# Finishing attention heads 0 to 3 inside the last units, starting the output projections on half of the heads, and starting the value projection from the first tile

## The chip, the core and the metric

The kernel runs on one core of a Trainium2 chip. The core has a matrix engine (PE, TensorE), three engines for vectors and scalars (DVE, ACT, POOL) and a queue engine (SP) that issues most transfers. Each engine works through its own list of instructions in order; semaphores tie the lists together. Times are device microseconds of one execution; lower is better.

## What is computed

The reference is a decoder of two layers over 512 tokens of width 1024. Layer 0 is a convolution module, layer 1 an attention that mixes three dilated windows; each is followed by a mixture of experts (64 experts, 8 for each token). Cut to what the change touches:

```python
def conv_module(x, w_in, b_in, w_dw, b_dw, ln_g, ln_b, w_out, b_out):
    ...
    h = jax.nn.silu(layernorm(h, ln_g, ln_b))
    return h @ w_out + b_out

def dilated_mixture_attention(x, positions, w_q, w_o, k, v):
    q = rotary((x @ w_q).reshape(B, S, N_GROUPS, HEADS_PER_GROUP, HEAD_DIM), positions)
    for g, (win, dil) in enumerate(WINDOW_DILATIONS):   # (128, 1), (512, 4), (2048, 16)
        o, lse = dilated_window_attention(q[:, :, g], k[:, :, g], v[:, :, g], dil, steps)
        ...
    wts = jax.nn.softmax(jnp.stack(lses, axis=2), axis=2)
    o = jnp.einsum("bsgh,bsghd->bshd", wts, jnp.stack(outs, axis=2))
    return o.astype(x.dtype).reshape(B, S, ATTN_OUT_WIDTH) @ w_o
```

Keys and values come from `x @ w_kv`. The result of each module is added to alpha times x and normalised (`layernorm`), then the experts run and a second norm follows.

## The kernel before

The 512 tokens are 4 tiles of 128 (`NT`), n = 0 to 3; the width is 8 pieces of 128 (`KT`). All engines run the same sequence of stages: the convolution, its output projection and norm round 0, the experts of layer 0 (a loop over blocks of 128 rows), norm round 1, the value projection, 16 attention units, the mixing of the heads, the attention's output projection and norm round 2, the experts of layer 1, norm round 3. PSUM has 8 banks (`PS[:, 0]` to `PS[:, 7]`).

**Norm rounds.** `norm_round(r)` on DVE normalises one tile after another (L876 residual, only in rounds 0 and 2; L884 statistics, L889 and L890 scale and shift, about 5 us in all). `x_T` on PE (L1233) transposes the tile; ACT and DVE copy it out. In round 1 ACT writes the rounded part `XTH` and DVE the remainder `XTL` (L861); DVE does this for tile n behind the norm of tile n+1.

**Value projection** (L1448 on PE). 24 pieces of weights, 3 buffers (`PIECES`). SP loads a piece into `RAW`, ACT rounds it into `PH` (L778), DVE takes the remainder `PL` (L1118). A product is three matmuls, so that float32 keeps its precision. PE takes piece by piece, in each all 4 tiles; it begins when all 4 tiles are transposed. Query and key pieces (48 more) follow on the same three buffers.

**Attention units.** Units 0 to 7 are the heads of the near window (one projection pair each), units 8 to 15 the heads of both dilated windows together (two pairs, `items(u)`). PE's list for unit u: `project(u+1)` (L1464), `probs_T(u-1)` (L1489, transposes of the probabilities), `scores(u)` (L1477), `pv(u-1)` (L1502). DVE rotates queries and keys, then masks the scores and takes the row maximum (L1165 to L1167), and copies the result of `pv` out (L1173). ACT copies the projections out (L799), computes the exponentials (L809) and copies the transposed probabilities (L814, L815).

**Mixing.** Near heads have tokens as rows in their order, dilated ("far") heads in another. So the row maxima and sums are exchanged through a small array in memory, `stat_ex`: SP issues two stores, waits, and issues two loads (L451 to L455), behind the last softmax. Then DVE and ACT work out the weights for all 8 heads (L1190 to L1200, L835), DVE scales the near and the far results (L1204), PE transposes them (L1530), ACT copies the near ones into `OT` (L840), DVE adds the far ones (L1213).

**Output projections.** `out_proj(l, ...)` runs after all of this for layer 1, and for layer 0 after all 8 pieces of the activated convolution (`s_z`, ACT L767). Each of the 64 float32 products (L1246; the trace shows two matmul records for one) reads its weights' chunk from `W`. Tile n uses banks 2(n % 2) and the next, so tile 2 waits for norm 0.

## Time and profile before

| | us |
| --- | --- |
| median of 3 runs | 2486.32 |
| lowest and highest | 2479.92, 2489.36 |
| the profiled execution's own time | 2482.47 |
| its span, first to last instruction | 2480.7 |
| PE busy | 2296.2 (93% of the span) |
| DVE busy | 1606.8 (65%) |
| ACT busy | 1076.4 (43%) |
| POOL busy | 684.8 (28%) |

The profile cuts the span into 40 slices. PE shows 9 tenths or more in nearly all of them; the lower ones lie at the start, at about slice 17 (around 1060 us), at slice 25 (around 1560 us) and after the second output projection. The stages that the change touches lie at 190 to 255 us, 1050 to 1219 us and 1540 to 1645 us.

### The profile page before, as it was taken

Reading aid. Unit: us, or ns where it says so; the run is one execution under the profiler, and the core shown is the slowest. Engines: PE = TensorE matmul, PEld = TensorE weight load, DVE = VectorE, ACT = ScalarE, POOL = GpSimd, SP = SyncE. Lnnn points to the kernel's source line nnn. Section 1 sums busy time; section 2 is a strip of 40 time slices with the busy share of each in tenths; the row PEclk is TensorE's granted clock in tenths of the full one; section 3 lists DMA queues with packets and bytes.
Section 4 is the critical chain, followed back from the end, with each engine's and each line's share of the span. In section 5 each row is a group of like instructions: output and inputs, shape, how many; then the busy total and the mean of one; then the engine's idle time right before and its main releaser. Section 6 shows DMA issues by size and latency. Waiting matters only on the chain.

```text
span 2480.7 us, 32934 instructions
## 1 busy us (share of the span) xinstructions
PE 2296.2 (93%) x9437; PEld 1633.7 (66%) x9437; DVE 1606.8 (65%) x1737; ACT 1076.4 (43%) x1215; POOL 684.8 (28%) x698
## 2 busy tenths in 40 slices
PE   7948889999999999869999999798999999999994
PEld 4413557767666667559988888554667777676673
DVE  4874557777767667552377787436677777776675
ACT  3651135555555555422243333112555555555552
POOL 3970213443434333200000000002233433334331
PEclk9969889999999999979999999889999999999997
DMA  6210359999999999633322222132999999999994
GB/s 216 68 34 0 127 202 346 371 366 375 360 350 362 365 345 372 209 134 93 94 77 69 79 83 83 56 119 70 339 366 367 368 364 363 367 372 355 360 364 142
DMA packets 197117, 592.57 MB, mean 239 GB/s; under 512 B 26605, under 2 KB 96277, under 8 KB 161732
## 3 DMA queue, kind: packets, MB, share of 16 engines
q1 hardware_dynamic: 165140, 517.92, 56.0%
q0 software_dynamic: 31920, 73.91, 12.2%
q8 instruction: 33, 0.54, 0.1%
q14 instruction: 24, 0.20, 0.0%
HBM read 579.16 MB, written 51.38 MB: 254 GB/s over the span
## 4 chain that ended last, share of the span: by engine, by line
PE 81%; DVE 6%; DMA 4%; ACT 1%; issue 1%; POOLq 0%; SPq 0%; DVEq 0%; ACTq 0%
PE PS L1355 29%; PE PS L1376 18%; PE PS L1464 11%; PE PS L1448 5%; PE PS L1246 5%; PE PS L1342 5%; DMA W<-in_exp_w_down 4%; PE PS L1280 2%; PE PS L1477 1%; PE PS L1364 1%; PE PS L1502 1%; PE PS L1326 1%; DMA acc<-BIG,IDXS 1%; PE PS L1299 1%; PE PS L1489 1%
## 5 line engine op out<-in xcount | busy, mean ns | idle before, releaser
L998 DVE TENSOR_TENSOR WL<-W,WH 128x2048 fp32r<-128x2048 f32 x276 | 621.3, 2293 | 197.3 <-ACT WH L679 185.9
L679 ACT ACTIVATE WH<-W 128x2048 fp32r<-128x2048 f32 x276 | 512.4, 1907 | 43.1 <-DVE IDX L976 42.4
L1376 PE MATMUL PS<-W,BIG 128*128 128x512 f32 x1104 | 498.6, 594 | 11.1 <-issue 5.0
L1355 PE MATMUL PS<-WH,XH 128*128 128x512 f32 x1104 | 446.6, 405 | 8.8 <-DVE XL L991 8.8
L1355 PE MATMUL PS<-WH,XL 128*128 128x512 f32 x1104 | 435.2, 394 | 0.0
L1355 PE MATMUL PS<-WL,XH 128*128 128x512 f32 x1104 | 432.6, 392 | 0.0
L589 POOL DMA_INDIRECT acc<-BIG,IDXS x138 | 259.1, 1878 | 471.3 <-issue 371.3
L1376 PEld LDWEIGHTS PS<-W,BIG 128*128 128x128 f32 x1104 | 199.2, 190 | 212.8 <-issue 205.1
L1355 PEld LDWEIGHTS PS<-WH,XH 128*128 128x128 f32 x1104 | 209.7, 190 | 48.2 <-DVE XL L991 9.6
L689 ACT ACTIVATE BIG<-PS 128x512 f32<-128x512 f32 x138 | 82.5, 598 | 362.5 <-PE PS L1376 362.5
L1355 PEld LDWEIGHTS PS<-WH,XL 128*128 128x128 f32 x1104 | 209.2, 189 | 46.0
L1355 PEld LDWEIGHTS PS<-WL,XH 128*128 128x128 f32 x1104 | 209.9, 190 | 39.7
L1016 DVE COPY BIG<-PS 128x512 f32<-128x512 f32 x138 | 95.4, 692 | 193.1 <-PE PS L1376 193.1
L528 POOL MEMSET BIG<- 128x2048 f32 x2 | 3.6, 1804 | 693.2 <-DVE X L890 601.4
L991 DVE TENSOR_TENSOR XL<-PS,XH 128x1024 fp32r<-128x1024 f32 x138 | 169.0, 1225 | 38.7 <-ACT XH L673 38.1
L574 POOL DMA_INDIRECT BIG<-xrows,IDXG x138 | 150.6, 1091 | 124.5 <-POOL IDXG L571 115.5
L673 ACT ACTIVATE XH<-PS 128x1024 fp32r<-128x1024 f32 x138 | 141.3, 1024 | 71.4 <-PE PS L1342 68.4
L1118 DVE TENSOR_TENSOR PL<-RAW,PH 128x1024 fp32r<-128x1024 f32 x72 | 87.5, 1217 | 114.7 <-ACT PH L778 114.7
L580 POOL COPY IDXS<-IDX 128x1 uint32 (+1 forms) x138 | 84.1, 609 | 250.9 <-issue 250.8
L1342 PEld LDWEIGHTS PS<-ident,BIG 128*128 128x128 f32 x1104 | 142.9, 188 | 15.8 <-issue 4.7
L1464 PE MATMUL PS<-XTH,PH 128*128 128x512 f32 x384 | 150.7, 393 | 0.0
L1464 PE MATMUL PS<-XTH,PL 128*128 128x512 f32 x384 | 149.6, 390 | 0.0
(233 smaller groups left out, 3110.2 us busy)
## 6 DMA issues: line engine op xcount, KB each, us to landing
W<-in_exp_w_gate SPq DMA_DIRECT2D x138, 1024.0 KB
W<-in_exp_w_up SPq DMA_DIRECT2D x138, 1024.0 KB
W<-in_exp_w_down SPq DMA_DIRECT2D x138, 1024.0 KB
RAW<-in_w_kv SPq DMA_DIRECT2D x48, 512.0 KB, 3.8
RAW<-in_attn_w_q SPq DMA_DIRECT2D x24, 512.0 KB, 3.7
W<-in_conv_w_in SPq DMA_DIRECT2D x8, 1024.0 KB, 11.4
acc<-BIG SPq DMA_DIRECT2D x9, 512.0 KB, 3.7
W<-in_conv_w_out SPq DMA_DIRECT2D x4, 1024.0 KB, 6.5
```

The source lines that it names most:

```text
L574: pool.indirect_dma_start(XG[:, s, :], None, xrows, bass.IndirectOffsetOnAxis(IDXG[:, s:s + 1], axis=0), bounds_check=T - 1, oob_is_err=Fa ...
L589: pool.indirect_dma_start(acc, bass.IndirectOffsetOnAxis(IDXS[0:r, s:s + 1], axis=0), YB[0:r, s, :], None, compute_op=ALU.add).then_inc(s_ ...
L673: A(XH[:, s, :], PS[:, 0:2, :].rearrange("p a t -> p (a t)"), ACT.Copy).then_inc(s_xh[l], 1)
L679: A(WH[:, s, c, :], W[:, 3 - 3 * s + c, :], ACT.Copy).then_inc(s_wh[l], 1)
L991: v.tensor_tensor(XL[:, s, :], PS[:, 0:2, :].rearrange("p a t -> p (a t)"), XH[:, s, :].bitcast(F32), ALU.subtract).then_inc(s_xl[l], 1)
L998: v.tensor_tensor(WL[s][:, c, :], W[:, 3 - 3 * s + c, :], WH[:, s, c, :].bitcast(F32), ALU.subtract).then_inc(s_wl[l], 1)
L1246: last = mm(PS[:, 2 * (n % 2) + h, :].rearrange("p (a b) -> p a b", a=2), lhs[:, k, n * P:(n + 1) * P], pair((key, 2 * h), k), start=(k == ...
L1342: last = nc.tensor.transpose(PS[:, k // 4, (k % 4) * P:(k % 4 + 1) * P], XG[:, s, :].rearrange("p (c k) -> p k c", k=KT)[:, k, :], ident[: ...
L1355: last = mm(PS[:, 3 + s, :].rearrange("p (a b) -> p a b", a=2), a, w, start=(k == 0 and i == 0), stop=(k == KT - 1 and i == 2))
L1376: last = mm(PS[:, 5 + h, :], HTm[:, s, k * P:(k + 1) * P], wd[:, k, h * 512:(h + 1) * 512], start=(k == 0), stop=(k == 1))
L1448: last = mm(PS[:, 4 * (c % 2) + n, :], a, w, start=(k == 0 and i == 0), stop=(k == KT - 1 and i == 2))
L1464: last = mm(PS[:, w, :], a, b[:, k, :], start=(k == 0 and t == 0), stop=(k == KT - 1 and t == 2))
```

## The change

1. **Layer 0 output projection.** Tiles 0 and 1 are worked on together, one piece k of the activations at a time, each as soon as that piece is ready. Tiles use four bank pairs (2n), so that no tile waits for a norm.
2. **Value projection.** The first three pieces are made (`PH`, `PL`) ahead of norm round 1 and are used tile by tile, as soon as that tile is transposed. The norm vectors' load (`ln_vectors(2)`) moves from piece 3 to piece 9 in SP's list.
3. **Heads 0 to 3 ("half 0").** Their weights, scaling and transposes are placed inside units 13 to 15. The statistics go out and come back in three exchanges, issued by POOL, the last with heads 4 to 7 alone. The near heads are scaled on ACT, the far ones on DVE.
4. **End of the units.** `scores(15)` uses banks 0 and 1 and stands ahead of `probs_T(14)`.
5. **Layer 1 output projection.** The products of tiles 0, 1 and 2 with heads 0 to 3 (24 of 64) stand between the transposes of heads 4 to 7; the other 40 follow.

The diff, cut to its core:

```diff
+        def xt_bank(q):
+
+            r, n = q // NT, q % NT
+            return 2 * n if r % 2 else 4 + 2 * (n % 2)
+
+        OT4 = BIG[:, 4096:8192].rearrange("p (m f t) -> p f m t", m=4, f=2)
+
+        MIX = 2 * 2 + 2 + NT
...
-                if j == PIECES:
+                if j == 3 * PIECES:
...
+            pool.wait_ge(s_p, 4 * 12)
+            pool.wait_ge(s_m, 12)
+            pool.dma_start(stat_ex[1].rearrange("(i j) c -> i j c", j=NT)[:, :, 0:8], statP[:, 1, :, 0:8]).then_inc(s_so, 16)
+            pool.wait_ge(s_so, 32)
+            pool.dma_start(statN[:, 1, :, 0:8], stat_ex[1].rearrange("(n p) c -> p n c", p=P)[:, :, 0:8]).then_inc(s_si, 16)
+            pool.wait_ge(s_p, 4 * 16)
+            pool.wait_ge(s_m, 16)
+            pool.dma_start(stat_ex[1].rearrange("(i j) c -> i j c", j=NT)[:, :, 8:16], statP[:, 1, :, 8:16]).then_inc(s_so, 16)
+            pool.wait_ge(s_so, 48)
+            pool.dma_start(statN[:, 1, :, 8:16], stat_ex[1].rearrange("(n p) c -> p n c", p=P)[:, :, 8:16]).then_inc(s_si, 16)
...
-            for j in range(PIECES - 1):
+            for j in range(PIECES):
                 piece_high(j)
+            norm_round(1)
             for j in range(n_v):
-                piece_high(j + PIECES - 1)
+                if j >= 1:
+                    piece_high(j + PIECES - 1)
...
+            def near_weigh(hf, n):
+                act.wait_ge(s_dve_w, MIX * hf + 5)
+                for h in range(4 * hf, 4 * hf + 4):
+                    o = O0[:, n, h * P:(h + 1) * P]
+                    last = A(o, o, ACT.Copy, scale=wt[:, 0, 3, n, h:h + 1])
+                last.then_inc(s_wn, 1)
+
+            def near_T(hf, n):
+                act.wait_ge(s_ot, 8 * hf + n + 1)
+                bank = 7 if hf == 0 else 6 + n % 2
+                A(OT4[:, hf, :, n * P:(n + 1) * P], PS[:, bank, :].rearrange("p (h t) -> p h t", h=4),
+                  ACT.Copy).then_inc(s_otn, 1)
...
+            def beside(u):
+
+                if u == 14:
+                    return lambda i: near_weigh(0, i - 1) if i else None
+                if u == 15:
+                    return lambda i: near_T(0, i)
+                return lambda i: None
...
+            def far_weigh(hf, n):
+                dve.wait_ge(s_dve_w, MIX * hf + 6)
+                o = O12[:, n, 512 * hf:512 * hf + 512].rearrange("p (h c) -> p h c", h=4)
+                v.tensor_tensor(o, o, wt[:, 1, 3, n, 4 * hf:4 * hf + 4].unsqueeze(2).broadcast_to([P, 4, P]),
+                                ALU.mult).then_inc(s_dve_w, 1)
+
+            def far_T(hf, n):
+                dve.wait_ge(s_otn, 4 * hf + 4)
+                dve.wait_ge(s_ot, 8 * hf + NT + n + 1)
+                bank = 7 if hf == 0 else 6 + n % 2
+                src = PS[:, bank, :].rearrange("p (h t) -> p h t", h=4)
+                dst = OT4[:, hf, :, :].rearrange("p h (i j) -> p h j i", j=NT)[:, :, n, :]
+                v.tensor_tensor(dst, dst, src, ALU.add).then_inc(s_ote, 1)
...
+            for u in range(16):
+                for k, (i, g) in enumerate(items(u)):
+                    rotate(i, g, u % 2, k, beside(u))
+                if u == 13:
+                    mix_least(0)
+            row_max(15)
+            far_T(0, 0)
+            far_T(0, 1)
+            pv_copy(14)
+            far_T(0, 2)
+            far_T(0, 3)
+            mix_least(1)
+            mix_weights(1, 0)
+            mix_weights(1, 1)
...
-            def out_proj(l, lhs, key):
-
-                for c in range(4):
-                    landed(pe, (key, c))
-                for n in range(NT):
-                    if n >= 2:
-                        pe.wait_ge(s_norm, 2 * NT * l + n - 1)
-                    for h in range(2):
-                        for k in range(KT):
-                            last = mm(PS[:, 2 * (n % 2) + h, :].rearrange("p (a b) -> p a b", a=2),
-                                      lhs[:, k, n * P:(n + 1) * P], pair((key, 2 * h), k), start=(k == 0), stop=(k == KT - 1))
-                    last.then_inc(s_mix[l], 1)
-                    if n >= 2:
-                        x_T(NT * (2 * l + 1) + n - 2)
+            def out_part(l, n, ks, hs=(0, 1)):
+
+                key = ("co", "ao")[l]
+                for h in hs:
+                    for k in ks:
+                        lhs = Y[:, k, :] if l == 0 else OT4[:, k // 4, k % 4, :]
+                        last = mm(PS[:, 2 * n + h, :].rearrange("p (a b) -> p a b", a=2),
+                                  lhs[:, n * P:(n + 1) * P], pair((key, 2 * h), k), start=(k == 0), stop=(k == KT - 1))
+                return last
+
+            def out_rest(l):
+
+                out_part(l, 2, range(4 if l else 0, KT)).then_inc(s_mix[l], 1)
+                x_T(NT * (2 * l + 1))
+                out_part(l, 3, range(KT)).then_inc(s_mix[l], 1)
+                x_T(NT * (2 * l + 1) + 1)
...
-            pe.wait_ge(s_z, KT)
-            out_proj(0, Y, "co")
+            for c in range(4):
+                landed(pe, ("co", c))
+            for k in range(KT):
+                pe.wait_ge(s_z, k + 1)
+                for n in range(2):
+                    last = out_part(0, n, (k,))
+                    if k == KT - 1:
+                        last.then_inc(s_mix[0], 1)
+            out_rest(0)
...
+            x_T(2 * NT)
+            x_T(2 * NT + 1)
             for n in range(NT):
+                pe.wait_ge(s_xta, 2 * NT + n + 1)
+                pe.wait_ge(s_xtv, 2 * NT + n + 1)
+                for j in range(PIECES):
+                    if n == 0:
+                        pe.wait_ge(s_pl, j + 1)
+                    last = v_part(j, n)
+                    if n == NT - 1:
+                        last.then_inc(s_v, 1)
+                if n + 2 < NT:
+                    x_T(2 * NT + n + 2)
...
+            def heads_T(hf, far, n):
+
+                f = NT * far + n
+                if far:
+                    pe.wait_ge(s_dve_w, MIX * hf + 6 + n + 1)
+                else:
+                    pe.wait_ge(s_wn, 4 * hf + n + 1)
+                if hf == 0:
+                    if f > NT:
+                        pe.wait_ge(s_ote, f - NT)
+                    elif f >= 1:
+                        pe.wait_ge(s_otn, f)
+                    bank = 7
+                else:
+                    if f < 2:
+                        pe.wait_ge(s_oe, 16)
+                        pe.wait_ge(s_ote, NT)
+                    elif f < 2 + NT:
+                        pe.wait_ge(s_otn, NT + f - 1)
+                    else:
+                        pe.wait_ge(s_ote, f - 1)
+                    bank = 6 + n % 2
+                o = (O0, O12)[far]
+                for h in range(4):
+                    last = nc.tensor.transpose(PS[:, bank, h * P:(h + 1) * P],
+                                               o[:, n, (4 * hf + h) * P:(4 * hf + h + 1) * P], ident[:, :])
+                last.then_inc(s_ot, 1)
...
+                        if u == 15:
+                            heads_T(0, 0, 2 * m + w)
...
+            for u in range(15):
+                project(u + 1)
                 if u >= 1:
                     probs_T(u - 1)
                 scores(u)
                 if u >= 1:
                     pv(u - 1)
+            scores(15)
+            heads_T(0, 1, 0)
+            probs_T(14)
+            heads_T(0, 1, 1)
+            pv(14)
+            heads_T(0, 1, 2)
             probs_T(15)
+            heads_T(0, 1, 3)
             pv(15)
-            for c in range(2 * NT):
-                o, n = (O0, O12)[c // NT], c % NT
-                pe.wait_ge(s_wts, c + 1)
-                if 2 <= c < NT + 2:
-                    pe.wait_ge(s_otn, 2 * (c - 1))
-                elif c >= 2:
-                    pe.wait_ge(s_ote, 2 * (c - 1 - NT))
-                for hf in range(2):
-                    for h in range(4):
-                        last = nc.tensor.transpose(PS[:, 4 + 2 * (c % 2) + hf, h * P:(h + 1) * P],
-                                                   o[:, n, (4 * hf + h) * P:(4 * hf + h + 1) * P], ident[:, :])
-                    last.then_inc(s_ot, 1)
+            pe.wait_ge(s_ote, NT)
+            for c in range(4):
+                landed(pe, ("ao", c))
+            out_part(1, 0, range(4))
+            heads_T(1, 0, 0)
+            heads_T(1, 0, 1)
+            out_part(1, 1, range(4), (0,))
+            heads_T(1, 0, 2)
+            heads_T(1, 0, 3)
+            out_part(1, 1, range(4), (1,))
+            heads_T(1, 1, 0)
+            heads_T(1, 1, 1)
+            out_part(1, 2, range(4), (0,))
+            heads_T(1, 1, 2)
+            heads_T(1, 1, 3)
+            out_part(1, 2, range(4), (1,))
             pe.wait_ge(s_ote, 2 * NT)
-            out_proj(1, OT, "ao")
+            for n in range(2):
+                out_part(1, n, range(4, KT)).then_inc(s_mix[1], 1)
+            out_rest(1)```

Three places show how the lists change. The names are those of buffers: `X` the tiles, `PL<-RAW,PH` the remainder of a weight piece, `XTL` the remainder of the transposed tile. First DVE before, at the end of norm round 1: the norm of the fourth tile, then the pieces.

```order
L884 BN_STATS bns<-X 128x6 x2
L886 BN_AGGR mv<-bns 128x2
L888 RECIPROCAL rstd<-std 128x1
L889 SCALAR_TENSOR_TENSOR X<-X,mv,LNG 128x1024
L890 SCALAR_TENSOR_TENSOR X<-X,rstd,LNB 128x1024
L861 TENSOR_TENSOR XTL<-PS,XTH 128x8x128 x2
L1112 TENSOR_SCALAR sinT<-sinT,sgn 32x512
L1118 TENSOR_TENSOR PL<-RAW,PH 128x1024 x6
```

DVE in the changed kernel, at the start of norm round 1, directly behind the last copy of the experts (L1066):

```order
L1066 COPY BIG<-PS 128x512
L1161 TENSOR_SCALAR sinT<-sinT,sgn 32x512
L1167 TENSOR_TENSOR PL<-RAW,PH 128x1024 x3
L934 BN_STATS bns<-X 128x6 x2
L936 BN_AGGR mv<-bns 128x2
L938 RECIPROCAL rstd<-std 128x1
L939 SCALAR_TENSOR_TENSOR X<-X,mv,LNG 128x1024
L940 SCALAR_TENSOR_TENSOR X<-X,rstd,LNB 128x1024
```

The first three pieces moved ahead of the first tile's norm. Next PE before, from `probs_T(14)` to `pv(15)`: transposes of probabilities (`PS<-ident,BIG`), scores and the product with the values (both `PS<-BIG`).

```order
L1489 MATMUL PS<-ident,BIG 128x128 x8
L1477 MATMUL PS<-BIG 128x128 x8
L1502 MATMUL PS<-BIG 128x128 x8
L1489 MATMUL PS<-ident,BIG 128x128 x8
L1502 MATMUL PS<-BIG 128x128 x8
```

PE in the changed kernel at the same place (L1617 is `scores(15)`, L1629 `probs_T`, L1642 `pv`, L1587 a `heads_T` of four far heads):

```order
L1617 MATMUL PS<-BIG 128x128 x8
L1587 MATMUL PS<-ident,BIG 128x128 x4
L1629 MATMUL PS<-ident,BIG 128x128 x8
L1587 MATMUL PS<-ident,BIG 128x128 x4
L1642 MATMUL PS<-BIG 128x128 x8
L1587 MATMUL PS<-ident,BIG 128x128 x4
L1629 MATMUL PS<-ident,BIG 128x128 x8
L1587 MATMUL PS<-ident,BIG 128x128 x4
L1642 MATMUL PS<-BIG 128x128 x8
```

The scores of unit 15 moved ahead of `probs_T(14)`, and four transposes of finished heads came in. Last PE before, from the heads' transposes to the end of the output projection (`PS<-W,BIG`):

```order
L1530 MATMUL PS<-ident,BIG 128x128 x64
L1246 MATMUL PS<-W,BIG 128x512 x48
L1233 MATMUL PS<-ident,X 128x128 x8
L1246 MATMUL PS<-W,BIG 128x512 x16
L1233 MATMUL PS<-ident,X 128x128 x16
```

PE in the changed kernel at the same place:

```order
L1329 MATMUL PS<-W,BIG 128x512 x8
L1587 MATMUL PS<-ident,BIG 128x128 x8
L1329 MATMUL PS<-W,BIG 128x512 x4
L1587 MATMUL PS<-ident,BIG 128x128 x8
L1329 MATMUL PS<-W,BIG 128x512 x4
L1587 MATMUL PS<-ident,BIG 128x128 x8
L1329 MATMUL PS<-W,BIG 128x512 x4
L1587 MATMUL PS<-ident,BIG 128x128 x8
L1329 MATMUL PS<-W,BIG 128x512 x28
L1319 MATMUL PS<-ident,X 128x128 x8
L1329 MATMUL PS<-W,BIG 128x512 x16
L1319 MATMUL PS<-ident,X 128x128 x16
```

Half of the 64 transposes left this place (they stand in units 15 and behind), and 20 of the 64 products stand ahead of the last of the others.

## Rows read from the trace of the kernel before

**Rows 1.** Stretches of the span: length, busy time (count) of each engine, granted clock, DMA share, GB/s.

```profile
1083.00:1219.00 136.00, 135.86 (x576) 127.84 (x577) 36.90 (x35) 29.25 (x33) 0.00 (x0) 0.98 0.33 101
1540.00:1586.00 46.00, 28.14 (x171) 26.07 (x169) 30.11 (x46) 14.26 (x36) 0.00 (x0) 0.78 0.45 140
```

**Rows 2.** Timeline (start, length, engine, line, [idle before]), end of the convolution.

```profile
190.85 5.75 ACT L767 ACTIVATE BIG<-BIG,vecT 128x512 f32<-128x512 f32 x8 [2.85 <-DVE BIG L1107]
196.65 43.24 PE L1246 MATMUL PS<-W,BIG 128*128 128x512 f32 x96 [10.77 <-ACT BIG L767]
```

**Rows 3.** Timeline, norm round 1 and the start of the value projection.

```profile
1054.65 1.53 SPq L445 DMA_DIRECT2D RAW<-in_w_kv  x3
1056.24 1.29 DVE L884 BATCH_NORM_STATS2 bns<-X 128x6 f32<-128x512 f32 x2 [9.48 <-DMA X<-acc]
...
1060.99 1.97 PE L1233 MATMUL PS<-ident,X 128*128 128x128 f32 x8 [15.05 <-DVE X L890]
...
1065.46 1.22 DVE L861 TENSOR_TENSOR XTL<-PS,XTH 128x1024 fp32r<-128x1024 f32 x1
...
1079.99 2.94 ACT L778 ACTIVATE PH<-RAW 128x1024 fp32r<-128x1024 f32 x3
...
1081.77 3.50 DVE L1118 TENSOR_TENSOR PL<-RAW,PH 128x1024 fp32r<-128x1024 f32 x3
...
1083.14 0.77 PE L1448 MATMUL PS<-PH,XTH 128*128 128x512 f32 x1 [4.11 <-DVE PL L1118]
```

**Rows 4.** DMA issues from 1055.5 to 1056.3: size, median us to landing.

```profile
RAW<-in_w_kv SPq DMA_DIRECT2D x2, 512.0 KB, 9.3
```

**Rows 5.** First projection of queries and keys: duration ns, first and last start.

```profile
L1464 PE MATMUL PS<-XTH,PH x384: 389/389/476, 1219.2 to 1539.7; 128*128 128x512 f32 x192
```

**Rows 6.** Timeline, units 14 and 15 and the exchange.

```profile
1540.41 1.03 PE L1489 MATMUL PS<-ident,BIG 128*128 128x128 f32 x8
1541.28 1.95 PE L1477 MATMUL PS<-BIG 128*128 128x128 f32 x16
...
1544.70 1.21 DVE L1165 TENSOR_TENSOR PS<-PS,mask_far 128x1024 f32<-128x1024 f32 x1
...
1547.41 0.47 ACT L809 ACTIVATE BIG<-PS,statP 128x256 f32<-128x256 f32 x1 [4.85 <-DVE statP L1167]
...
1549.39 1.97 PE L1489 MATMUL PS<-ident,BIG 128*128 128x128 f32 x8 [4.38 <-ACT BIG L809]
...
1551.16 3.62 PE L1477 MATMUL PS<-BIG 128*128 128x128 f32 x16
...
1559.50 0.37 SPq L451 DMA_DIRECT2D stat_ex<-statN  x1
...
1561.80 3.47 PE L1502 MATMUL PS<-BIG 128*128 128x128 f32 x16 [1.17 <-ACT BIG L815]
...
1565.30 0.69 DVE L1173 COPY BIG<-PS 128x512 f32<-128x512 f32 x1 [7.21 <-PE PS L1502]
1565.91 0.18 DVE L1190 TENSOR_TENSOR wt<-statN 128x32 f32<-128x32 f32 x1
```

**Rows 7.** Timeline, mixing, all 8 heads.

```profile
1569.23 6.90 DVE L1204 TENSOR_TENSOR BIG<-BIG,wt 128x1024 f32<-128x1024 f32 x6
...
1578.32 7.92 DVE L1213 TENSOR_TENSOR BIG<-BIG,PS 128x512 f32<-128x512 f32 x8
```

**Rows 8.** Timeline of PE, output projection of layer 1.

```profile
1586.30 43.03 PE L1246 MATMUL PS<-W,BIG 128*128 128x512 f32 x96 [2.02 <-DVE BIG L1213]
...
1630.04 13.90 PE L1246 MATMUL PS<-W,BIG 128*128 128x512 f32 x32
1643.78 1.91 PE L1233 MATMUL PS<-ident,X 128*128 128x128 f32 x16
```

**Rows 9.** Timeline: last indirect transfer of POOL, and SP's loads that wait for it.

```profile
1048.71 1.38 POOL L589 DMA_INDIRECT acc<-BIG,IDXS  x1 [2.50 <-issue]
1052.84 1.76 SPq L412 DMA_DIRECT2D X<-acc  x4
```

More of the change, by code:

```diff
@@ L769, in _ @@
             moe(0)
-            norm_round(1)
             def piece_high(j):
@@ L1441, in _ @@
                 pe.wait_ge(s_pl, j + 1)
[L1442 to L1448 removed]
+                for n in range(NT):
+                    last = v_part(j, n)
                 last.then_inc(s_v, 1)
@@ L1510, in _ @@
             pe.wait_ge(s_veh, 12)
-            for u in range(16):
-                if u < 15:
-                    project(u + 1)
+            for u in range(15):
+                project(u + 1)
                 if u >= 1:
```

171 lines of the change are left out of this document (91 added, 80 removed).

## The prediction

> **What bounds the kernel now.** I read the page first: PE is busy for 93% of the span, so a change pays only where PE waits or where its list gets shorter. Then I cut the span into stretches. In the value projection PE has 135.86 us of work in 136; between the last projection and the output projection it has 28.14 in 46, at a granted clock of 0.78 [rows 1]. The timelines of the three touched places then show what ends each wait. The convolution's output projection starts at 196.65, when the last of 8 activations ends [rows 2]. The value projection starts at 1083.14, behind four norms and the first pieces; its first tile was normed by 1060.99 [rows 3]. The output projection of layer 1 starts at 1586.30, 45.9 us after PE ended its last projection at 1540.41 [rows 6, 8]. The experts' loops, most of the span, are not touched; what the three places save should reach the end one for one, because every later stage hangs on PE's or the norm's end.
>
> **Part 1, layer 0 output projection: 5 us.** Eight activations take 5.75 us [rows 2], 0.72 from start to start, so the first is ready 7 x 0.72 = 5.0 us ahead of the last. A piece k gives PE four products. 32 records took 13.90 us [rows 8], so a product (two records) takes 0.87 and four 3.5, five times as long as one activation: once PE has begun it is never starved. The number of products is the same. Norm 0 now comes after tile 1 instead of tile 0, but two norms of about 7 us lie under the 14 us of tile 2 and more under tile 3; the end, tile 3's norm, moves with tile 3. Gain 5.0; bounds 3.5 (a slow start of the clock lasting longer because the work ahead is further away) and 5.0.
>
> **Part 2, value projection: 2 us.** Norm round 1 now stands behind three pieces on DVE. SP issues them right behind X, from 1054.65 to 1056.18 [rows 3], and the later two take 9.3 us to land in the median [rows 4], so the third is there at about 1065.4. ACT's rounding takes 1.0 and DVE's remainder 1.2 more [rows 3], with hand-overs 1067.8. Norm 0, which began at 1056.24, is 11.6 us later. From its start the first transposed tile took 4.8 (1060.99), and its remainder begins 9.2 and ends 10.4 after the start (1066.68) [rows 3]: now 1078.3. PE has tile 1's transposes to finish first, until 1079.1. There the projection starts, 4.0 us earlier than 1083.14. But two transposed tiles (8 transposes each, 1.03 as in [rows 6]) now lie inside it: 2.1 us. A tile's share of three pieces is 18 matmuls, at 135.86 / 576 = 0.236 [rows 1] 4.2 us, and with its transposes 5.3, while DVE brings a tile every 5.7 us (a norm 4.5, a remainder 1.2) and has a lead of one tile. Piece 4 is needed 4.2 us after tile 3's share begins; its buffers come free after the first third (1.4), and rounding and remainder take 2.2: just in time. The queries' projection, now at 1219.2 [rows 5], comes at about 1217.2. Gain 2; bounds -2 (pieces land 2 us later, or the last tiles wait for DVE) and +5 (pieces 3 us earlier). This is the part where the change works against itself: it frees PE of the wait for four norms and puts the norms behind a load.
>
> **Part 3, end of the units and layer 1 output projection: 19 us.** E is the end of PE's last projection, 1540.4. Four groups of four transposes (half of 1.03 each) are inserted in `project(15)`, three ahead of E: E moves to 1542.0 [rows 6]. The work on heads 0 to 3 on DVE (six steps, about 6 us) lies in unit 14, where DVE has some 4.5 of 26 us free; it comes late by about 1.5 us, and PE wants its pieces two steps (11 us) later, so I price it at nothing; without that cover it would cost those 1.5.
>
> From E: the rotation ends and the row maximum starts at +4.3 as before (1544.70) [rows 6]. `scores(15)` no longer waits for unit 14's softmax, +5.2 to +7.1; row maximum of 14, a copy, row maximum of 15 (2.6 each) end at +10.2. Softmax 14 is over at +8.9, `probs_T(14)` at +10, its copies at +11.3, softmax 15 at +13.2, i.e. 1555.2; before 1559.50, where the exchange begins [rows 6]. Then transposes of probabilities, copies, `heads_T(0,1,3)` and `pv(15)`: PE is free at +18.6, and I add 1.5 because `pv(15)` took 3.47 instead of 1.95 at the lower clock [rows 6]: B = 1562.1.
>
> Behind B PE has 64 products, 56.6 us (1586.30 to 1643.78 less one transposed tile of 0.9) [rows 8], eight groups of transposes 4.1 and one tile 0.9: 61.6. If it never waits, tile 3 ends at 1623.7, against 1643.78: 20.1 less.
>
> Does it wait? The exchange of heads 4 to 7 starts at 1555.2 on POOL. SP's took 1559.50 to 1565.9 at most (DVE went on at 1565.91, maybe behind its copy) [rows 6], so 6.4 or less for two transfers. POOL's last indirect transfer took 4.1 from its start to the release of SP (1048.71 to 1052.84) [rows 9], so twice 8.2. It holds 512 short lines and now meets the six 1 MB weight loads in flight. Lower bound 5, upper 20; I take 10, near the indirect row. DVE starts mixing at 1565.3; half the weights take as long as all (3.3 us, 1565.91 to 1569.23, since they are small steps) [rows 6, 7], the near ones 2.2. ACT scales 4 x 128 columns for a tile; its 256-column step takes 0.47 [rows 6], so a step costs 0.25 to 0.47, a tile 1.0 to 1.9. The first near tile is ready at 1568.7, and PE asks for it after 8 products, 1562.1 + 7 + 0.7 = 1569.8. The transposed near heads are copied only when all four tiles are scaled, at 1571.5 to 1575.1 plus 0.6; PE asks for the first at 1569.8 + 1.0 + 3.5 = 1574.3. So there is no wait at ACT's low price and 1.4 us at its high one; I take 1. The far side (DVE scaling 4 x 0.6, adding 4 x 0.99 [rows 7]) has 4 us of room. Gain 20.1 - 1 = 19; bounds 10 (exchange 20 us: 9 us more wait) and 23 (no loss of clock, exchange hidden). Behind the exchange on DVE stands only the mixing, on POOL nothing until the experts, and SP loses four transfers.
>
> A rule speaks against this part. Before, no transfer of POOL's queue ran beside DVE's work on the mix, and no row shows what one does there. The Trainium skill (SBUF — State Buffer, "Who interferes with whom") says that POOL cannot write the descriptors of its transfers while DVE runs in a two-port mode, as a float32 copy within SBUF does, and that such a transfer goes from some 0.6 to 3.1 us. The DVE steps in this stretch read PSUM, so I expect it not to bite; by its figure the exchange would take 5 us more (an estimate from that page), and the part would gain about 14.
>
> **Sum.** 5 + 2 + 19 = 26. Against the profiled execution's own 2482.47 (1.8 beyond its span) that is 2456.5; against the median of the runs, 3.9 higher, 2460.3. I forecast 2458, between the two. Within 0.5% (12.4 us) a measurement of this kernel can hardly tell a difference from none.
>
> **Rivals.**
> 1. *The forecast: all three parts, 20 to 32 us less.* Chance 0.72: 2450 to 2466.
> 2. *The exchange becomes PE's wait.* DVE waits for POOL's transfers, PE for DVE and ACT. It bites from about 10 us; at 20 it costs 9: total gain 16 to 20, time 2466 to 2472. For: no row shows such a transfer, and the weight loads are in flight. Against: the indirect one took 4.1. Chance 0.12.
> 3. *The early start of the values costs instead of paying, and unit 14 overloads DVE.* Pieces land at 1068, tile 1's norm comes late, PE waits 4 us in the values and some 5 in `project(15)`: gain 12 to 16, time 2468 to 2474. For: DVE's margin in unit 14 is negative by itself. Chance 0.08.
> 4. *No change that can be measured.* The parts gain 5 and 2, and the third only what the earlier softmax gives (4), because PE stays cold or waits between all the small groups: 11 us less, 2475. Against: 24 products of 0.87 are real work taken into the wait, and nothing in the rows starves them all. Chance 0.05.
> 5. *Slower.* POOL's exchange alone: the part's gain is gone at 10 + 19 = 29 us, and all of it at 36; from about 48 us the kernel is slower by 0.5%. At 50 us it would take 2500. Chance 0.01. Another 0.02 for a gain over 32 (colder clock before than I count, 2445).
>
> **Numbers.** The range reaches from 2448 to 2470: it holds the forecast, half of rival 2 and part of 3. Faster by over 0.5%: 0.92; within: 0.06; slower: 0.02.
>
> **What the profile of the changed kernel would show.** Part 1 is right if the first product of layer 0 starts 5 us ahead of the last activation's end, with no gaps. Part 2: the norm's first statistics at about +11.6 and the first value product at 4 us earlier relative to the end of the experts; wrong if norm 0 starts later or PE has gaps between the tiles' shares. Part 3: PE's stretch from the last projection to the end of tile 3's products 81 to 84 us instead of 103.4; softmax 15 some 13 us after the last projection; POOL's two transfers in 10 us. The prediction fails if the products on heads 0 to 3 have gaps among them, if `project(15)` waits for `PL`, or if the transposes between them run at half clock throughout.

## The result, and the profile after

The changed kernel takes 2452.8 us (median of 4 runs, 2450.3 to 2456.2) against 2485.0 for the kernel before (4 runs, 2479.9 to 2489.4): a ratio of 0.987, 95% interval 0.986 to 0.989. The time is in the range (2448 to 2470), 5 us under the forecast of 2458. The profiled execution has a span of 2451.5 us against 2480.7, 29.3 us less.

I cut both traces at the same points of the program. Starts and ends are read from PE's rows, lengths are differences of them (us):

| stretch | before | after | difference |
|---|---|---|---|
| start of the span to the first product, layer 0 output projection | 196.65 | 191.80 | -4.9 |
| from there to the last tile of that projection | 57.69 | 58.93 | +1.2 |
| routing of layer 0 | 94.23 | 95.03 | +0.8 |
| experts' loop of layer 0 | 704.27 | 705.43 | +1.2 |
| SP's load of `X` to the first value product | 30.30 | 25.62 | -4.7 |
| value projection | 136.03 | 136.82 | +0.8 |
| projections of queries and keys with the units among them | 321.40 | 323.26 | +1.9 |
| last of those to the last tile of layer 1's output projection | 103.21 | 77.91 | -25.3 |
| routing, experts' loop and end of layer 1 | 836.96 | 836.67 | -0.3 |

Windows of the changed kernel's trace first (length, then busy time and count of PE, PEld, DVE, ACT, POOL, then granted clock, DMA share, GB/s). The first row begins with the layer 0 output projection, the second with the value projection; the others answer to [rows 1], and the last is the router's stretch.

```profile
191.80:201.80 10.00, 10.00 (x17) 4.23 (x18) 3.22 (x6) 6.07 (x8) 0.00 (x0) 0.69 0.01 2
...
1076.81:1086.81 10.00, 10.00 (x46) 8.26 (x45) 9.07 (x14) 2.42 (x4) 0.00 (x0) 0.91 0.00 1
...
1077.00:1213.00 136.00, 135.98 (x591) 127.82 (x591) 45.66 (x47) 32.71 (x38) 0.00 (x0) 0.99 0.31 95
...
1536.70:1554.80 18.10, 14.60 (x125) 13.70 (x124) 14.04 (x17) 8.10 (x24) 0.72 (x1) 1.00 1.00 317
1554.80:1614.80 60.00, 59.54 (x170) 28.38 (x169) 26.69 (x47) 10.24 (x29) 0.77 (x1) 1.00 0.04 11
1614.80:1640.00 25.20, 22.95 (x107) 17.79 (x106) 11.28 (x29) 4.93 (x7) 1.80 (x1) 0.73 0.82 292
```

The 46 us with 28 us of PE work in them have become 18 with 14.6, at full clock, and the output projection behind them has no hole but one of 0.46 us. In the trace before, the same ten microseconds had a clock of 0.82 and 19 records at the start of the output projection, and 0.77 and 35 records at the start of the value projection.

The timeline of the changed kernel (start, length, engine, operation, idle before), at the three places, answers to [rows 2], [rows 3, 9] and [rows 6, 8]:

```profile
190.84 5.75 ACT L788 ACTIVATE BIG<-BIG,vecT 128x512 f32<-128x512 f32 x8 [2.85 <-DVE BIG L1157]
191.80 44.48 PE L1329 MATMUL PS<-W,BIG 128*128 128x512 f32 x96 [5.93 <-ACT BIG L788]
...
1063.61 1.06 ACT L798 ACTIVATE PH<-RAW 128x1024 fp32r<-128x1024 f32 x1 [0.22 <-DMA RAW<-in_w_kv]
...
1065.84 1.28 DVE L934 BATCH_NORM_STATS2 bns<-X 128x6 f32<-128x512 f32 x2
...
1076.81 0.78 PE L1534 MATMUL PS<-PH,XTH 128*128 128x512 f32 x1
...
1536.50 0.39 PE L1601 MATMUL PS<-XTH,PL 128*128 128x512 f32 x1
...
1545.74 1.09 PE L1629 MATMUL PS<-ident,BIG 128*128 128x128 f32 x8 [1.74 <-ACT BIG L833]
...
1550.07 0.72 POOL L639 DMA_DIRECT2D stat_ex<-statP  x1 [81.54 <-ACT BIG L833]
...
1552.92 2.05 PE L1642 MATMUL PS<-BIG 128*128 128x128 f32 x16
1554.81 7.03 PE L1329 MATMUL PS<-W,BIG 128*128 128x512 f32 x16
...
1555.97 0.77 POOL L641 DMA_DIRECT2D statN<-stat_ex  x1 [5.18 <-DMA stat_ex<-statP]
1558.38 0.18 DVE L1236 TENSOR_TENSOR wt<-statN 128x16 f32<-128x16 f32 x1 [2.68 <-DMA statN<-stat_ex]
...
1560.24 2.45 ACT L852 ACTIVATE BIG<-BIG,wt 128x128 f32<-128x128 f32 x8 [0.65 <-DVE wt L1250]
...
1562.74 0.66 PE L1587 MATMUL PS<-ident,BIG 128*128 128x128 f32 x4 [0.46 <-ACT BIG L852]
1563.23 3.60 PE L1329 MATMUL PS<-W,BIG 128*128 128x512 f32 x8
...
1614.80 1.91 PE L1319 MATMUL PS<-ident,X 128*128 128x128 f32 x16
```

The first product of layer 0 starts 1.0 us after the first activation. The norm's first statistics stand 14.7 us behind SP's load of `X` (1051.18), against 3.4 before [rows 3, 9]. PE goes from the last projection (it ends at 1536.89) to the first attention product in 17.9 us, and the exchange takes 8.3 us from POOL's start to DVE's first mixing step. PE's last steps of the units and its products on heads 0 to 3, started at 1554.81, cover the exchange and the scaling behind it but for 0.46 us.

### The profile page after: what moved, and what is told of

Same layout as the page of the kernel before. It is cut to its first block, busy times and chain, and to the rows that moved or that the text cites. A ratio compares the mean times of both kernels' runs of the same rounds, so it can differ in the third digit from the quotient of the medians.

```text
span 2451.5 us, 32999 instructions
## 1 busy us (share of the span) xinstructions
PE 2286.8 (93%) x9437; PEld 1623.4 (66%) x9437; DVE 1604.3 (65%) x1753; ACT 1085.8 (44%) x1251; POOL 696.8 (28%) x704
## 4 chain that ended last, share of the span: by engine, by line
PE 79%; DMA 8%; DVE 5%; ACT 1%; issue 1%; SPq 0%; POOLq 0%; POOL 0%; DVEq 0%; ACTq 0%
PE PS L1443 27%; PE PS L1464 18%; PE PS L1601 11%; DMA W<-in_exp_w_down 6%; PE PS L1534 6%; PE PS L1329 4%; PE PS L1430 4%; PE PS L1368 2%; PE PS L1452 1%; PE PS L1642 1%; PE PS L1617 1%; PE PS L1414 1%; DMA acc<-BIG,IDXS 1%; PE PS L1387 1%; PE PS L1348 1%
## 5 line engine op out<-in xcount | busy, mean ns | idle before, releaser
L1464 PE MATMUL PS<-W,BIG 128*128 128x512 f32 x1104 | 499.3, 595 | 10.5 <-issue 4.5
L594 POOL DMA_INDIRECT acc<-BIG,IDXS x138 | 265.8, 1926 | 464.7 <-issue 391.6
L1464 PEld LDWEIGHTS PS<-W,BIG 128*128 128x128 f32 x1104 | 199.2, 190 | 213.4 <-issue 204.8
L1066 DVE COPY BIG<-PS 128x512 f32<-128x512 f32 x138 | 95.4, 692 | 194.6 <-PE PS L1464 193.4
L1167 DVE TENSOR_TENSOR PL<-RAW,PH 128x1024 fp32r<-128x1024 f32 x72 | 87.7, 1218 | 121.7 <-ACT PH L798 121.3
L1601 PE MATMUL PS<-XTH,PH 128*128 128x512 f32 x384 | 151.0, 393 | 0.0
L704 ACT ACTIVATE BIG<-PS 128x256 f32<-128x256 f32 x138 | 53.1, 385 | 219.0 <-PE PS L1443 219.0
L1601 PE MATMUL PS<-XTH,PL 128*128 128x512 f32 x384 | 149.7, 390 | 0.0
## 6 DMA issues: line engine op xcount, KB each, us to landing
RAW<-in_w_kv SPq DMA_DIRECT2D x48, 512.0 KB, 3.8
RAW<-in_attn_w_q SPq DMA_DIRECT2D x24, 512.0 KB, 3.8
acc<-BIG SPq DMA_DIRECT2D x9, 512.0 KB, 3.7
```

Source lines behind the costliest of these rows:

```text
L594: pool.indirect_dma_start(acc, bass.IndirectOffsetOnAxis(IDXS[0:r, s:s + 1], axis=0), YB[0:r, s, :], None, compute_op=ALU.add).then_inc(s_ ...
L1464: last = mm(PS[:, 5 + h, :], HTm[:, s, k * P:(k + 1) * P], wd[:, k, h * 512:(h + 1) * 512], start=(k == 0), stop=(k == 1))
L1601: last = mm(PS[:, w, :], a, b[:, k, :], start=(k == 0 and t == 0), stop=(k == KT - 1 and t == 2))
```

## The experiments

The numbers below are of single profiled runs unless an interval is given; kernels that ran together had a kernel before at 2481 to 2486 us beside them. Since the experts' loops alone vary by some 7 us between runs (last section), a part is judged by the length of its own stretch, and the total is told beside it. A stretch varies as well. The one from PE's last projection to the last tile of layer 1's output projection is unedited in seven runs (the changed kernel, its repetition, parts 1 and 2 taken back, part 3 alone, and two with the pieces behind two norms): 77.9 to 80.1 us, the middle one 78.75. The changed kernel's own profile is the shortest of them, so a difference told against its 77.9 is 0.8 us larger than one against the middle.

**Part 1 taken back.** PE waits for all eight pieces once.

```diff
+            pe.wait_ge(s_z, KT)
             for k in range(KT):
-                pe.wait_ge(s_z, k + 1)
```

> The changed kernel, but the output projection of layer 0 waits for all 8 activations again (bank pairs and order of the products kept). Theory (the early start is what pays in part 1): tile 3's products end at 254.3 instead of 250.7, 3.6 us later, and the time rises by 3.6, to about 2456.8. Rival (the bank pairs, which take away the wait for norm 0, are what pays): no change, 250.7.

2459.6 us. The first product starts at 196.26 and the last tile's transposes at 254.59, against 191.80 and 250.72 in the changed kernel, and an end of 248.2 to 250.3 in the ten other runs that kept part 1. The early start is what pays: 3.9 us against the changed kernel, 4.7 against the middle of the eleven ends with part 1 (249.8). The bank pairs, which this run keeps, pay nothing that shows: it ends at 254.59, the kernel before at 254.34.

**Part 2 taken back.** The norms stand ahead of the pieces on DVE and ACT, PE transposes all four tiles and then projects.

```diff
+            norm_round(1)
             for j in range(PIECES):
                 piece_low(j)
-            norm_round(1)
```

> The changed kernel with part 2 undone: norms first, then the pieces, then the value projection of all tiles. Theory (part 2 by itself is worth the 3.9 us that the two traces show from SP's load of X to the first query projection, 166.4 against 162.5): 166.4 again, time up by 3.9. Rival (it is worth nothing by itself, the 3.9 came from the rest): 162.5 and no change of time.

2456.3 us. From SP's load of `X` to the first projection of queries it takes 166.46 us, as before the change (166.33), against 162.45. That is 4.0 us, twice its term in the sum, of this pair. All the runs say 3.3: the three without part 2 have 165.7 to 166.5 (mean 166.2), the eight that have it as in the changed kernel 161.7 to 163.8 (mean 162.8).

**Part 2 with the pieces behind two norms.** The projection from the first tile on stays, but two norms no longer stand behind the load, on DVE and in the same way on ACT.

```diff
-            for j in range(PIECES):
-                piece_low(j)
             norm_round(1)
...
+                    if r == 1 and n == 1:
+                        for j in range(PIECES):
+                            piece_low(j)
```

> The changed kernel, with the first three pieces taken between the second and the third norm of round 1, on ACT and on DVE. In the changed kernel DVE stands idle for 16.5 us until the first piece is there, while X has landed. Theory (the place of the pieces ahead of all norms gives most of the early start back): the first value product starts 15 us behind SP's load of X instead of 25.6, tile 3's share ends 6 to 7 us earlier, and the time falls by 5 to 7, to about 2447. Rival (PE's list is the bound from the first share on, and its clock falls in the gaps between the shares): under 2 us gained.

2444.1 us. The timeline of this kernel (its line numbers are shifted by one or two):

```profile
1051.31 1.29 DVE L935 BATCH_NORM_STATS2 bns<-X 128x6 f32<-128x512 f32 x2 [8.98 <-DMA X<-acc]
...
1061.67 3.49 DVE L1171 TENSOR_TENSOR PL<-RAW,PH 128x1024 fp32r<-128x1024 f32 x3
...
1063.03 0.77 PE L1536 MATMUL PS<-PH,XTH 128*128 128x512 f32 x1 [0.39 <-DVE PL L1171]
...
1069.82 1.10 PE L1321 MATMUL PS<-ident,X 128*128 128x128 f32 x8 [1.11 <-DVE X L941]
...
1075.56 1.09 PE L1321 MATMUL PS<-ident,X 128*128 128x128 f32 x8 [0.16 <-DVE X L941]
```

The values begin 15.1 us behind the load of `X` and not 25.6; DVE's lead is then too small, so PE waits 1.11 and 0.16 us for tiles 2 and 3, and the projection is 2.7 us longer. What stays is 154.6 us for the stretch, 7.8 under the changed kernel. That is what the order of norms and pieces costs, where the prediction saw the change work against itself.

**Part 3 without the early products.** All the transposed heads first, then every product.

```diff
-            out_part(1, 0, range(4))
-            heads_T(1, 0, 0)
...
+            for far in range(2):
+                for n in range(NT):
+                    heads_T(1, far, n)
             pe.wait_ge(s_ote, 2 * NT)
             for n in range(2):
-                out_part(1, n, range(4, KT)).then_inc(s_mix[1], 1)
+                out_part(1, n, range(KT)).then_inc(s_mix[1], 1)
```

> The changed kernel, but all 64 products of layer 1's output projection stand behind the last transposed heads again; halves, placement of heads 0 to 3 and the order of the units are kept. Theory (the 24 products of 0.86 us lie in a wait for the mixing of heads 4 to 7): PE waits some 16 us between pv(15) and the products, tile 3 ends at 1631 instead of 1614.8, the time rises by 15 to 18. Rival (what pays in part 3 is the work on heads 0 to 3 inside the units, the chain of the second half is short): up by less than 6.

2455.4 us, which is only 2.6 over the changed kernel and misses the total. Its timeline and, in the last row, the window that answers to the last one above:

```profile
1546.55 2.05 PE L1642 MATMUL PS<-BIG 128*128 128x128 f32 x16
1555.30 1.98 PE L1587 MATMUL PS<-ident,BIG 128*128 128x128 f32 x8 [6.71 <-ACT BIG L852]
1559.08 3.81 PE L1587 MATMUL PS<-ident,BIG 128*128 128x128 f32 x16 [1.79 <-ACT BIG L858]
1563.38 2.09 PE L1587 MATMUL PS<-ident,BIG 128*128 128x128 f32 x8 [0.50 <-DVE BIG L1264]
1566.69 43.64 PE L1329 MATMUL PS<-W,BIG 128*128 128x512 f32 x96 [1.22 <-DVE BIG L1264]
...
1624.80:1650.00 25.20, 22.95 (x137) 18.07 (x136) 12.14 (x35) 5.58 (x9) 2.53 (x2) 0.93 0.83 292
```

PE waits 6.71, 1.79, 0.50 and 1.22 us where the changed kernel has products, and runs its transposes at the lower clock (1.98 us for the eight that take 1.04). The stretch from the last projection to the last tile is 94.3 us against 77.9: 16.4 more, as the theory said. The rest of the program happened to be shorter: the routing of layer 1, an unchanged list, took 87.8 us and not 93.1, since the granted clock of its first 25.2 us was 0.93 and not 0.73 (137 records and not 107); the two experts' loops were 7.1 us shorter together. Both runs took their unit steps up to `pv(15)` alike (the slow `pv(14)` told of below is in neither), so the 16 us are a fair difference. That the stage lost them is measured; the total of one run couldn't show it.

**The last exchange on SP's queue**, behind the weight loads that stand there.

```diff
             for i in range(n_first, n_first + SLOTS):
                 load_chunk(i)
+            sp.wait_ge(s_p, 4 * 16)
+            sp.wait_ge(s_m, 16)
+            sp.dma_start(stat_ex[1]..., statP[:, 1, :, 8:16]).then_inc(s_so2, 16)
+            sp.wait_ge(s_so2, 16)
+            sp.dma_start(statN[:, 1, :, 8:16], stat_ex[1]...).then_inc(s_si2, 16)
```

> The changed kernel, with the last exchange of statistics (heads 4 to 7) issued by SP behind its weight loads instead of by POOL. In the changed kernel it takes 8.6 us from the last softmax (1549.77) to the first step of the mixing (1558.38), and PE waits 0.5 us for scaled near heads. Theory (PE is not held up by the exchange, its list is the bound): exchange some 3 us shorter, PE's stretch from its last projection to tile 3's end 77.9 before and 77 to 78 now. Rival (the exchange on POOL is the bound of the second half): 3 us shorter.

2453.3 us. Its timeline:

```profile
1548.09 1.79 SPq L464 DMA_DIRECT2D stat_ex<-statP  x1
...
1556.34 0.37 SPq L466 DMA_DIRECT2D statN<-stat_ex  x1
...
1558.23 0.17 DVE L1241 TENSOR_TENSOR wt<-statN 128x16 f32<-128x16 f32 x1 [4.20 <-DMA statN<-stat_ex]
...
1561.42 0.66 PE L1592 MATMUL PS<-ident,BIG 128*128 128x128 f32 x4 [1.25 <-ACT BIG L854]
```

Expected shorter, it is longer: 10.1 us instead of 8.3, of which the store alone 8.3. PE waits 1.25 and 0.52 us, and its stretch is 79.5 us, forecast 77 to 78. My theory that POOL's path makes the exchange slow fell here.

**The exchange done twice**, on POOL; the mixing waits for the second.

```diff
+            pool.wait_ge(s_si, 48)
+            pool.dma_start(stat_ex[1]..., statP[:, 1, :, 8:16]).then_inc(s_so, 16)
+            pool.wait_ge(s_so, 64)
+            pool.dma_start(statN[:, 1, :, 8:16], stat_ex[1]...).then_inc(s_si, 16)
...
-                dve.wait_ge(s_si, 32 + 16 * hf)
+                dve.wait_ge(s_si, 32 + 32 * hf)
```

> The changed kernel, with the last exchange done a second time by POOL behind the first, with the same data; the mixing waits for the second. It costs 8.3 us more until the mixing starts. Theory (there is next to no room behind the exchange: PE already waits 0.5 us for ACT's scaled near heads): PE's stretch from its last projection to tile 3's end grows from 77.9 to 85.5 to 86.5. Rival (the products between the transposes leave room): under 4 us more.

2451.8 us. The timeline of its POOL, and of PE:

```profile
1542.47 0.72 POOL L639 DMA_DIRECT2D stat_ex<-statP  x1 [81.52 <-ACT BIG L837]
1548.42 0.77 POOL L641 DMA_DIRECT2D statN<-stat_ex  x1 [5.23 <-DMA stat_ex<-statP]
1551.29 0.72 POOL L643 DMA_DIRECT2D stat_ex<-statP  x1 [2.11 <-DMA statN<-stat_ex]
1553.70 0.77 POOL L645 DMA_DIRECT2D statN<-stat_ex  x1 [1.69 <-DMA stat_ex<-statP]
...
1559.13 0.66 PE L1591 MATMUL PS<-ident,BIG 128*128 128x128 f32 x4 [3.33 <-ACT BIG L856]
...
1560.86 5.23 PE L1333 MATMUL PS<-W,BIG 128*128 128x512 f32 x8
```

The first store takes 5.95 us from its start to the next transfer, the identical second one 2.41. So the exchange costs 8.8 us the first time and, with DVE going on at 1555.93, 4.6 the second. PE's stretch grows by 6.9 us to 84.8: its waits are 3.33 and 0.52 instead of 0.46, products that took 3.60 take 5.23 at the lower clock after the wait, and `pv(14)` took 3.06 instead of 1.95. So nearly all added time comes out at PE. How much room there was depends on `pv(14)`: where it took 1.95 us, PE waits already behind an exchange of 8.3; where it was slow, as here, the first product starts 1.5 us later and PE doesn't wait behind the single exchange (so in part 1 taken back and in both runs of the pieces behind two norms). Against those runs (78.75 to 78.9 us) the 5.2 us of longer exchange delay the first transposes by 3.5 and lengthen the stretch by 6.0; 1.6 of that are the eight products of 5.23 us.

**`scores(15)` behind unit 14's transposes again**, as in the kernel before.

```diff
-            scores(15)
             heads_T(0, 1, 0)
             probs_T(14)
+            scores(15)
             heads_T(0, 1, 1)
```

> The changed kernel, with scores(15) behind probs_T(14) again, as in the kernel before. Theory (the softmax of unit 15 and with it both the exchange and pv(15) hang on these scores): softmax 15, the exchange and the first product come 4 us later, PE's stretch from its last projection to tile 3's end grows from 77.9 to about 82. Rival (that order is worth nothing, since DVE's and ACT's steps follow one another anyhow): under 1 us.

2456.9 us. PE in its timeline:

```profile
1541.79 1.70 PE L1629 MATMUL PS<-ident,BIG 128*128 128x128 f32 x8 [3.52 <-ACT BIG L833]
1543.27 3.03 PE L1617 MATMUL PS<-BIG 128*128 128x128 f32 x16
1550.16 1.09 PE L1587 MATMUL PS<-ident,BIG 128*128 128x128 f32 x4 [3.86 <-DVE BIG L1264]
1551.04 3.62 PE L1642 MATMUL PS<-BIG 128*128 128x128 f32 x16
```

The stretch is 86.0 us, 8.1 more (7.3 against the middle of the unedited ones) and not 4: the direction was right, the size about double. PE has two waits of 3.5 and 3.9 us instead of 1.7 and 1.2, and the scores and `pv(14)` behind them take 3.03 and 3.62 instead of 1.95 each. Of the 8.1 us, 4.4 are the longer waits, 2.8 are those two steps at the lower clock, and the rest is spread over small steps.

**The weight loads behind the exchange.** SP issues its first four loads and holds the rest until the exchange is over.

```diff
             for i in range(n_first, n_first + SLOTS):
+                if i == n_first + 4:
+                    sp.wait_ge(s_si, 48)
                 load_chunk(i)
```

> The changed kernel, with SP's loads of the shared experts' gate and up weights (1 MB each) held until the last exchange is over; it is issued by POOL as in the changed kernel. There the first of its two transfers took 5.9 us from issue to landing, and 2.4 when it was repeated later with no load in flight. Theory (the store waits behind the weight loads on the DMA engines): exchange from the last softmax to the mixing 8.6 before, 5 to 6 now; PE's stretch falls by no more than its 0.5 us of wait, and tile 3 ends as before. Rival (the first transfer on POOL is slow by itself, for its 512 short lines): 8.6 again.

2451.1 us. Its timeline:

```profile
1546.98 0.72 POOL L641 DMA_DIRECT2D stat_ex<-statP  x1 [81.55 <-ACT BIG L835]
1549.66 0.77 POOL L643 DMA_DIRECT2D statN<-stat_ex  x1 [1.97 <-DMA stat_ex<-statP]
...
1554.09 0.17 DVE L1238 TENSOR_TENSOR wt<-statN 128x16 f32<-128x16 f32 x1
...
1560.15 1.04 PE L1589 MATMUL PS<-ident,BIG 128*128 128x128 f32 x8
```

The store takes 2.7 us instead of 5.9, and the mixing waits for DVE's own copy and no longer for the exchange. The windows of the two stores, the changed kernel's first (the columns are those of the windows above):

```profile
1550.07:1555.97 5.90, 5.33 (x39) 4.33 (x38) 3.49 (x4) 1.08 (x2) 0.72 (x2) 1.00 1.10 350
...
1546.98:1549.66 2.68, 2.68 (x21) 2.68 (x21) 0.97 (x3) 0.00 (x0) 0.72 (x1) 0.78 0.17 39
```

The slow store lies in full DMA traffic (350 GB/s), the quick one in next to none (39): what makes the store slow is the company of the weight loads. PE gains nothing that can be put down to it: the stretch is 78.8 us, with `pv(14)` at the lower clock (3.08 us), and from the first attention product it is 59.3 against 60.0, without the wait of 0.46. But part 1 taken back and both runs of the pieces behind two norms, with the loads where the changed kernel has them and the same slow `pv(14)`, also take 59.3 without that wait.

**Part 3 alone, timed.** The edits of the first two experiments together.

> The changed kernel with parts 1 and 2 undone, so part 3 alone. Theory (the parts add up): the stages of part 1 and 2 as in the two undoing runs, PE's stretch from its last projection to tile 3's end 78 to 80; time 3.6 to 4.3 and 3.9 us above the changed kernel, 2460 to 2461, ratio to the kernel before 0.990. Rival (parts 1 and 2 shift the loads or the clock for part 3): more than 3 us off that.

2459.2 us (4 runs, 2457.1 to 2463.6), ratio 0.991, interval 0.988 to 0.993, against a kernel before of 2482.2. So of the 2482.2 less 2449.0 that the whole change gave in that job, 23.0 are part 3 and 10.2 the two others. Their own stretches gave 7 to 8 us (3.9 to 4.7 and 3.3 to 4.0); with runs of one kernel up to 6.6 us apart the parts add up as far as medians can tell.

**Pieces behind two norms and the exchange on SP, timed.**

> The changed kernel with both edits: the first pieces between the second and third norm, and the last exchange on SP. Theory: the first is worth the 7.8 us of its stage that its own run showed, the second 0 to 0.5: time 8 us under the changed kernel's 2452.8, about 2444.5, ratio to the kernel before about 0.984. Rival (PE waits less where it is fed earlier, but the experts' loops take it back): no better than 0.987.

2447.0 us (4 runs, 2443.7 to 2449.9), ratio 0.986, interval 0.984 to 0.988, against 2481.3. The forecast's 0.984 lies at the edge of the interval, the rival's 0.987 inside it, so the total decides for neither. The stages repeat what the single runs showed: 155.4 us from the load of `X` to the queries, and 79.5 for PE's last stretch, with a store of 8.4 us in SP's queue.

**The pieces behind two norms, and the changed kernel again, timed in one job.**

> The kernel with the first pieces between the second and third norm once more, timed in rounds beside the changed kernel. Its stage was 7.8 us shorter. Theory: median 7 to 9 us under the changed kernel of the same rounds. Rival (the experts' loops, which differ by several us from run to run with the same lists, hide it): under 3 us.

> The changed kernel once more, timed in the same rounds as the others. Every theory: ratio to the kernel before 0.987 to 0.989.

2446.5 us (2445.7 to 2448.6; ratio 0.985, interval 0.983 to 0.987) and 2449.0 us (2445.5 to 2451.0; 0.986, 0.984 to 0.988), 4 runs each, against 2482.2. The stretch from the load of `X` to the queries is 154.5 and 161.7 us, 7.2 apart, but the medians are 2.5 apart and the intervals overlap. In the profiled pair the two experts' loops took 704.3 and 724.7 us in the one, 701.9 and 722.7 in the other: 4.5 us of it back. The stage is shown; that this version beats the changed kernel in total is not.

## Why the prediction was right

**Direction and cause.** All three parts did what they were taken for, and each was undone by itself: 3.9, 4.0 and, for the early products and the scores alone, 16.4 and 8.1 us in their stretches. The forecast was 26 us less; the profile shows 29.3 and the medians 32.2. In the profile the three touched stages give 30.9 (3.6, 3.9 and 23.4), and the untouched ones take 1.7 back. So direction and mechanism were right, and the sum was 5 us too small: part 1 gave 1.4 less, part 2 gave 1.9 more and part 3 gave 4.4 more. That the errors of parts 1 and 2 nearly cancel is luck.

**Part 1, 5 us forecast, 3.6 measured.** The start came 4.85 us earlier as counted (seven activations), and PE was never starved. 1.2 us went in the first ten microseconds of the projection: a granted clock of 0.69 instead of 0.82, the bound that I had put at 3.5. The same list took 57.3 to 58.9 us over all runs, so that loss belongs to no edit; against the middle of the runs part 1 is worth 4.7.

**Part 2, 2 us forecast, 4.0 measured (3.3 over all runs).** The pieces came when I had them (ACT's third rounding at 1063.6, 12.4 us behind the load of `X`; forecast 12.6 to the landing), norm 0 moved by 11.3 us, where 11.6 were forecast, and PE had no gap among the tiles' shares. The term that was mis-sized is the transposes inside the projection, 2.1 us: they are there, but the projection only grew by 0.8, since it now starts behind a wait of 2.6 us instead of 4.1 and ran its first ten microseconds at a clock of 0.91 instead of 0.77. The start itself was 0.7 us earlier than I had it.

**Part 3, 19 us forecast, 23.4 measured** (25.3 less 1.9 for the transposes in the units). That is just outside my bounds of 10 to 23, and PE's stretch of 77.9 us is under the 81 to 84 that I gave as its sign; the seven unedited runs have at most 80.1. The chain behind it came as worked out: the last exchange starts 13.2 us after PE's last projection, and softmax 15 was forecast to end at +13.2. From the end of PE's last projection before (+0) I had the first attention product at +21.7; it stands at 1.9 + 17.9 = 19.8. 1.5 us of that were the slow `pv(15)` that I had added, and it took 2.05. That this run was spared them is luck: in four of the seven unedited runs `pv(14)` takes 3.05 to 3.62 us and not 1.95 (a granted clock of 0.62 and not 1.00 during it, in part 1 taken back and in the changed kernel), behind the same two waits of 1.7 and 1.2, and the first product comes 19.4 to 20.8 us after the last projection instead of 17.9. No run here settles what decides between the two. From the product to the last tile I had 62.6, and it takes 60.0: the wait is 0.5 and not 1, four groups of eight transposes take 0.87 each and not 1.03 (0.6), and the products run at full clock throughout, where those before had 0.97 over their stretch and 0.84 in its first ten microseconds (1.5). Of the two prices for ACT's scaling the low one held: eight steps in 2.45 us, 0.31 each, against my 0.25 to 0.47. DVE's load in unit 14 cost nothing to be seen (PE's longest wait within the units is 0.16 us); the units grew by 1.9 us, where three groups of four at half of 1.03 made 1.6.

**The exchange** (rival 2) took 8.3 us, between the 5 and 20 of my bounds and near the 10 taken. Its threshold of about 10 was nearly right: at 8.3 PE waits 0.46 or not at all, by `pv(14)`, and with 13.5 in the doubled run 3.9. I had taken the price near the row of POOL's indirect transfer and named the weight loads beside it; what sets it is the loads, and not that POOL issues it (2.7 us without them, 5.9 with them, 8.3 in their own queue).

**The rule that spoke against it.** By the Trainium skill (SBUF — State Buffer, "Who interferes with whom") a two-port step of DVE holds up the descriptors of POOL's transfers, and I had estimated 5 us more by it. Its figures of 0.6 and 3.1 us stand in another section of that page, "A bandwidth-pool intuition that's wrong (but worth ruling out)". The traces don't show the effect here, and don't test it: DVE's four steps during the slow store (1550.07 to 1555.97) are two copies out of PSUM and two additions with one operand in PSUM, as I had expected. POOL's own part is 0.72 and 0.77 us in the slow store (5.9 us) and the quick one (2.4) alike, and what moved the price was where the weight loads stood.

**A slip in the chances.** The rivals' chances add up to 0.94 for faster by over 0.5%, 0.05 for within and 0.01 for slower; the closing line has 0.92, 0.06 and 0.02.

## What to carry to other kernels

When an engine waits for the last piece of a chain, look for work of the same engine that needs only the first half, and order the next engine's chain before the filler: the filler was worth 16 us here, the order of one small step 7 to 8, a third of it through the clock that the closed gap preserves. In an in-order queue, put what is ready ahead of what hangs on a load: three pieces ahead of the norms cost 7 to 8 us of stage time that two norms ahead of them gave back. Judge an edit worth under 10 us by the length of its own stage, and take the middle of several runs even there; one run's total can hide it.

## What the runs showed of the hardware that I had not expected

- The time of a store of 512 short lines went with the DMA traffic around it. From POOL's queue it took 2.4 us at 7 GB/s (the second exchange of the doubled run, and heads 0 to 3 in the changed kernel), 2.7 at 39 (loads held back), 3.1 at 119 (`scores(15)` behind, where the store comes later) and 5.9 at 350 GB/s, in all nine runs that have it there beside the loads. In SP's queue behind the loads it took 8.3 and 8.4. The load that follows it took 2.4 us in the changed kernel, 2.9 and then 2.2 in the doubled run, and 1.9 on SP.
- One small step is quick or slow in different runs of one list: `pv(14)` took 1.95 us in three of the seven unedited runs and 3.05 to 3.62 in the four others, behind the same waits of 1.7 and 1.2 us.
- One and the same list of PE takes different times in different runs. The routing of layer 1 took 87.8 to 93.8 us; its start was at a granted clock of 0.93 in the shortest and 0.73 in the changed kernel, and in both PE waits 2.25 us for a norm, until 7.7 us into it. Why the clock rose earlier in the one, no run here settles.
- The experts' loops vary as well without an edit: 698.4 to 705.4 us in layer 0 and 716.2 to 724.7 in layer 1, over 14 profiled runs. They carry most of the spread of the totals. The clock doesn't make it: it is 0.99 over the loop in every run, and the DMA engines are 98% busy. The same 245.0 MB of layer 0 move at 351 GB/s in the shortest and 347 in the longest, the same 251.7 MB of layer 1 at 351 and 347. So what differs is the pace of the transfers and not the clock; why they are slower in some runs, and whether PE is held by them step by step, no run shows.
